# The v projection of a hybrid SSD / gMLP step by four weight tiles at once, and the order of the convolution tiles around it

## What is computed

```python
h = rms_norm(x, norm_w) * (1 + scale[:, None]) + shift[:, None]
proj = h @ w_in
xbc_raw, z_m, dt_raw, u_raw, v_raw, z_g, gl_m, gl_g = jnp.split(proj, _split_points(IN_SIZES), axis=-1)
y_m, h_fin = _ssd_branch(xbc_raw, dt_raw, z_m, h0, ...)   # xbc = silu(_dwconv(xbc_raw, conv_w, conv_b)), 5 taps
y_g = _gmlp_branch(u_raw, v_raw, z_g, ...)                # v = layer_norm(gelu(v_raw))
merged = sigmoid(gl_m) * (y_m @ w_out_m) + sigmoid(gl_g) * (y_g @ w_out_g)
return x + gate[:, None] * (merged @ w_out), h_fin
```

## Time and profile before

| | us |
|---|---|
| median of 3 runs | 1444.05 (1443.5 to 1444.36) |
| the profiled execution, its own time | 1443.57 |
| its span, first to last instruction | 1441.8 |
| PE busy | 1425.8, 99% of the span |
| DVE, POOL, ACT busy | 975.0, 1023.6, 474.2 |
| mean granted TensorE clock | 0.998 of full speed |

### The profile page before, as it was taken

The page is one execution under the profiler, slowest core; times in us unless marked ns, Lnnn a source line. Parts: engine busy times, 40 slices in busy tenths (PEclk is TensorE's granted clock), DMA queues, the critical chain, the costliest instruction groups (busy, mean ns, idle before and its releaser), DMA issues.

```text
span 1441.8 us, 27057 instructions
## 1 busy us (share of the span) xinstructions
PE 1425.8 (99%) x10191; PEld 1388.0 (96%) x10191; DVE 975.0 (68%) x1454; ACT 474.2 (33%) x1086; POOL 1023.6 (71%) x1421
## 2 busy tenths in 40 slices
PE   8999999999999999999999999999999999999997
PEld 5999998999999999999999999989999999999997
DVE  5865576674767678988879676567566876867234
ACT  4331223313766333001243323241257661320122
POOL 2688875596555589998859897658765556979772
PEclk9999999999999999999999999999999999999999
DMA  9112333113565565444332232421346565453222
GB/s 358 60 64 78 129 106 121 63 62 116 152 193 183 158 253 194 152 151 138 115 132 74 78 122 93 134 63 59 103 127 181 170 189 186 161 187 118 74 74 88
DMA packets 113838, 189.54 MB, mean 131 GB/s; under 512 B 12736, under 2 KB 76352, under 8 KB 112320
## 3 DMA queue, kind: packets, MB, share of 16 engines
q1 hardware_dynamic: 42736, 138.34, 29.1%
q10 hardware_dynamic: 70992, 49.63, 11.5%
HBM read 169.79 MB, written 18.15 MB: 130 GB/s over the span
## 4 chain that ended last, share of the span: by engine, by line
PE 96%; DVE 2%; DMA 1%; SPq 0%; ACT 0%; issue 0%; DVEq 0%; ACTq 0%
PE acc L600 78%; PE acc L567 6%; PE X L840 2%; PE X L805 2%; PE X L567 1%; PE X L825 1%; PE X L872 1%; DMA ada_pre<-in_wada 1%; PE X L851 1%; PE X L759 1%; DVE cv L1620 1%; PE X L649 0%; PE acc L718 0%; DVE h_pre L1473 0%; DVE xr L1936 0%; PE X L812 0%
## 5 line engine op out<-in xcount | busy, mean ns | idle before, releaser
L510 POOL CAST w_hi<-w_st 128x256 fp32r<-128x256 f32 x704 | 419.8, 610 | 396.1 <-issue 182.6
L514 POOL TENSOR_TENSOR w_lo<-w_st,w_hi 128x256 fp32r<-128x256 f32 x704 | 641.5, 921 | 0.0
L600 PE MATMUL acc<-h_hi,w_hi 128*128 128x320 f32 x1744 | 406.3, 314 | 0.7 <-ACT h_hi L1045 0.7
L600 PE MATMUL acc<-h_lo,w_hi 128*128 128x320 f32 x1744 | 397.8, 309 | 1.1 <-DVE h_lo L1467 1.1
L600 PE MATMUL acc<-h_hi,w_lo 128*128 128x320 f32 x1744 | 397.2, 309 | 0.0
L600 PEld LDWEIGHTS acc<-h_hi,w_hi 128*128 128x128 f32 x1744 | 288.6, 188 | 10.5 <-issue 7.8
L600 PEld LDWEIGHTS acc<-h_lo,w_hi 128*128 128x128 f32 x1744 | 291.3, 188 | 1.8 <-DVE h_lo L1467 1.7
L600 PEld LDWEIGHTS acc<-h_hi,w_lo 128*128 128x128 f32 x1744 | 291.7, 188 | 0.0
L1620 DVE SCALAR_TENSOR_TENSOR cv<-raw,convw_sb,cv 128x642 f32<-128x642 f32 x128 | 134.9, 1054 | 4.5
L1387 DVE SCALAR_TENSOR_TENSOR ada_acc<-ada_st,sc,ada_acc 128x512 f32<-128x512 f32 x112 | 104.2, 969 | 1.8
L1141 ACT ACTIVATE cvt<-cv 128x642 f32<-128x642 f32 x32 | 23.8, 743 | 158.4 <-DVE cv L1620 158.4
(11 more groups left out here) (257 smaller groups left out, 2474.8 us busy)
## 6 DMA issues: line engine op xcount, KB each, us to landing
w_st<-in_wts SPq DMA_DIRECT2D x176, 512.0 KB, 3.6
cum_bc<-cum_dram ACTq DMA_DIRECT2D x80, 256.0 KB, 4.9
ada_st<-in_wada SPq DMA_DIRECT2D x33, 512.0 KB, 4.3
ex_bc<-ex_dram ACTq DMA_DIRECT2D x64, 128.0 KB, 3.2
ada_pre<-in_wada SPq DMA_DIRECT2D x15, 512.0 KB, 9.7
mga_dram<-c_buf SPq DMA_DIRECT2D x16, 320.0 KB, 6.0
xf<-xf_dram SPq DMA_DIRECT2D x4, 1280.0 KB, 7.7
mga<-mga_dram SPq DMA_DIRECT2D x2, 2560.0 KB, 10.0
```

The source lines that it names most:

```text
L510: nc.gpsimd.tensor_copy(quarter(w_hi, slot, q), quarter(w_st, slot, q)).then_inc(s_pool, 1)
L514: nc.gpsimd.tensor_tensor(quarter(w_lo, slot, q), quarter(w_st, slot, q), f(quarter(w_hi, slot, q)), ALU.subtract).then_inc(w_split, 1)
L600: last = mm(a[:, hf, 0:n1], w[:, s, cols], x[:, k, hf * HALF:hf * HALF + n1], start=(k == 0 and n == 0), stop=(k == KC - 1 and n == 2))
```

## The change

- **v by four.** v's tiles are taken in two groups of four, in slots 3 to 6 and 20 to 23. 512 weight columns move in each matmul; a slot has a quarter of the rows of all four tiles, 2 blocks x 5 chunks x 3 = 30 matmuls. Each chunk of tokens fills a whole bank: chunk 4 X[1] or X[3], chunks 0 and 1 one accumulator, chunks 2 and 3 the other one. The chunks are taken in the order 4, 0, 1, 2, 3, and the wait for an accumulator stands ahead of its first chunk. A slot of v now waits for all four quarters of its weights.
- **ACT** applies the gelu bank by bank (`v_gelu`), 5 instructions of 512 columns a group, as each chunk of the last slot ends.
- **Convolutions.** CONV_AT becomes slots 0 to 2 and 7 to 19. For convolutions 4 to 15 (AHEAD) DVE does the first tap of convolution i + 1 ahead of the closing product of convolution i. ACT's order stays.
- **Transposes and bursts.** X sets in slots 15 to 22 at step 2; bursts 0, 1, 2 in slots 17 to 19 at step 3, the other 18 in slots 24 to 29.

```diff
-V_AT = (3, 4, 9, 10, 15, 16, 22, 23)
+V_AT = (3, 4, 5, 6, 20, 21, 22, 23)
+VQ = 4
+AHEAD = tuple(range(NRAW + 1, NCONV))
-A_AT = [(18 + a, 2) for a in range(7)] + [(25 + a // 3, 2 + 3 * (a % 3)) for a in range(14)]
-X_AT = [(p + 2, 4) for p in CONV_AT[8:14]] + [(24, 3), (24, 6)]
-V_BANK = (1, 1, 3, 1)
+A_AT = [(17 + a, 3) for a in range(3)] + [(24 + n // 8, n % 8 + 1) for n in (1 + 13 * a // 5 for a in range(18))]
+X_AT = [(p + 3, 2) for p in CONV_AT[8:16]]
+V_BANK = (1, 3)
...
+            bank = X[V_BANK[n % NQ]]
+            if i == 0:
...
+                if n % NQ == 1:
+                    pe.wait_ge(cum_ready, t // NT + 1)
+                    pe.wait_ge(s_out, NU * (t // NT) + 2)
+            pe.wait_ge(w_split, WQ * (t + 1))
...
+                for c in (NCH - 1,) + tuple(range(NCH - 1)):
+                    key = t0 if c < 2 else ("v", t0)
+                    if k == 0 and c in (0, 2):
+                        acc_ready(key)
+                    out = bank if c == NCH - 1 else acc_of(key)[:, c % 2, :]
+                    for m, (w, x) in enumerate(((w_hi, h_hi), (w_lo, h_hi), (w_hi, h_lo))):
+                        last = mm(out[:, :].rearrange("p (t n) -> p t n", t=VQ), x[:, k, P * c:P * (c + 1)],
+                                  w[:, t % 2, :].rearrange("p (t k n) -> p k t n", t=VQ, n=P)[:, kk, :, :],
+                                  start=(k == 0 and m == 0), stop=(k == KC - 1 and m == 2))
...
+                    last = A(v_tok[:, VQ * q:VQ * (q + 1), c, :], bank[:, :].rearrange("p (g n) -> p g n", n=P),
+                             ACT.Gelu_apprx_tanh)
+                    if c in (1, NCH - 2):
+                        free(key, last)
...
             for i in range(NCONV):
...
-                own.link(TS(o, r[:, PAD:PAD + CW], w[:, PAD:PAD + 1], w[:, TAPS:TAPS + 1], ALU.mult, ALU.add))
+                if i not in AHEAD:
+                    first_tap(i)
                 for tap in (0, 1, 3, 4):
...
+                if i + 1 in AHEAD:
+                    first_tap(i + 1)
                 dve.wait_ge(cvt_ready, NCONV * L + i + 1)
...
-                for a in {10: (0, 1), 11: (2,), 12: (3,), 13: (4,), 14: (5, 6), 15: (7, 8)}.get(i, ()):
+                for a in {11: (0, 1), 13: (2,), 15: (3,)}.get(i, ()):
                     a_unit(a)
```

More of the change, by code:

```diff
@@ L66, in accumulator_uses @@
             t = L * NT + p
-            if p in V_AT[1::2]:
+            if p in V_AT and p not in V_AT[::VQ]:
                 uses[t] = uses[t - 1]
@@ L71, in accumulator_uses @@
             at = 1 - at
+            if p in V_AT:
+                take(("v", t))
+                at = 1 - at
             if p == 0:
@@ L542, in acc_ready, with v_tile @@
                 pe.wait_ge(acc_free[at], n)
[L544 to L554, removed]
-                    pe.wait_ge(hpre_ready, 8 * (ready[2] + 1))
[L556 to L559, removed]
+        def v_tile(t, i, ready=None, hooks=()):
+            t0 = t - i
+            n = NQ * (t // NT) + V_AT.index(t0 % NT) // VQ
+            bank = X[V_BANK[n % NQ]]
+            if i == 0:
+                if n % NQ == 0 and ready is not None:
+                    pe.wait_ge(hpre_ready, 8 * (ready[2] + 1))
+                if n % NQ == 1:
+                    pe.wait_ge(cum_ready, t // NT + 1)
+                    pe.wait_ge(s_out, NU * (t // NT) + 2)
+            pe.wait_ge(w_split, WQ * (t + 1))
+            step = 0
+            for kk in range(2):
+                k = 2 * i + kk
                 if ready is not None:
@@ L562, in v_tile @@
                         pe.wait_ge(r, 8 * ready[2] + k + 1)
[L563 to L571, removed]
+                for c in (NCH - 1,) + tuple(range(NCH - 1)):
[7 more added lines that the diff above has]
+                                  start=(k == 0 and m == 0), stop=(k == KC - 1 and m == 2))
+                    if kk == 1 and c == NCH - 2:
                         last.then_inc(tile_done, 1)
+                    elif k == KC - 1:
+                        last.then_inc(v_done, 1)
+                    step += 1
                     for at, hook in hooks:
-                        if (at == 2 * i + 1 and c == 2) or (at == 2 * i + 2 and c == NCH - 1):
+                        if (5 * at + 3) // 4 == step:
                             hook()
@@ L1141, in conv_tanh, with v_gelu @@
                 A(cvt[:, 0:CW], cv[:, i % 2, 0:CW], ACT.Tanh).then_inc(cvt_ready, 1)
+            def v_gelu(q, t):
+                t0 = t - VQ + 1
+                own.link(A(warm[:, :], eps_sb[:, :], ACT.Gelu_apprx_tanh))
+                for i, c in enumerate((NCH - 1,) + tuple(range(NCH - 1))):
+                    key = t0 if c < 2 else ("v", t0)
+                    if i < NCH - 1:
+                        act.wait_ge(v_done, (NCH - 1) * (NQ * L + q) + i + 1)
+                    else:
+                        act.wait_ge(tile_done, t + 1)
+                    bank = X[V_BANK[q]] if i == 0 else acc_of(key)[:, c % 2, :]
+                    last = A(v_tok[:, VQ * q:VQ * (q + 1), c, :], bank[:, :].rearrange("p (g n) -> p g n", n=P),
+                             ACT.Gelu_apprx_tanh)
+                    if c in (1, NCH - 2):
+                        free(key, last)
+                evacuated(act, ("v", t0))
+                act.sem_inc(v_made, 1)
             def copies(p):
@@ L1151, in _ @@
                 t = T0 + p
-                if L == 0 or p >= RAWT:
+                if p in V_AT and V_AT.index(p) % VQ == VQ - 1:
+                    v_gelu(V_AT.index(p) // VQ, t)
+                elif L == 0 or p >= RAWT:
                     act.wait_ge(tile_done, t + 1)
                 if p in V_AT:
[L1155 to L1162, removed]
                     if L > 0 and p == RAWT + 1:
@@ L1607, in a_unit, with first_tap @@
                 last.then_inc(xw_ready, 1)
-            for i in range(NCONV):
-                ch = (i + 8) % NCONV
+            def first_tap(i):
                 if L > 0 and i < NRAW:
```

31 lines of the change are left out of this document (18 added, 13 removed).

## The result

| | us |
|---|---|
| median of 4 runs of the changed kernel | 1466.60 (1465.19 to 1469.04) |
| median of before beside them, 4 runs | 1443.78 (1443.41 to 1444.36) |
| ratio | 1.0155, 95% interval [1.0143, 1.0167] |
| the profiled execution of after, its own time; its span | 1469.04; 1467.3 |
| mean granted TensorE clock in that execution | 0.991 |

The change makes the kernel 22.8 us slower. The profiled execution is 2.4 us above the median, and its opening, which the change doesn't touch, is 2.3 us longer than before up to slot 3 of layer 0 (that slot starts at 65.12 and not at 62.86). In that opening PE's clock was at half twice, 16.5 to 20.0 and 40.4 to 43.8 us, where the profile of before shows it full. The other three runs, with a mean granted clock of 0.993, are shorter. I leave these 2.3 us out of what follows and count from slot 3 on.

A forecast was written before the change was run, and what follows sets the result against it. PE's own time was taken to bound the kernel. Wider matmuls -6.4, copy-out waits +4.9 and +14.7, and late weight quarters +1.3 gave +14.5 on 1444.05, hence 1458.5 us; the range was 1443 to 1467.5.

The forecast's parts named there:

- rival 3: Matmuls of 512 columns in v's slots are no cheaper than two of 256; +20.9 us, 1465; chance 0.06.
- rival 4: PE's clock halves behind a 5 to 8 us pause in slot 20: 4.5 us a layer, +23.5, 1467.5; chance 0.08.
- Wider matmuls: PE, 16 slots of v: 30 matmuls at 0.227 us, read off a line through three sizes, save 6.4 us.
- The loop: DVE and ACT, first tap to first tap: closing product and handover add 0.87, giving 7.55 us in layer 0, 8.04 in layer 1.
- Waits for the copy-out: PE waits for ACT's accumulator copy-outs up to slot 19's, mostly in slot 20: 4.9 us in layer 0, 14.7 in layer 1.
- All four quarters: Slots 4 and 5 of layer 1 start late behind POOL's last weight quarter: 1.3 us for both, bounds 0 and 2.1.
- The cover that I named for slot 20: In slots 20 to 23 the copy-out wait covers the wait for POOL's weight quarters, so no time was added there.
- Rival 1: The convolution loop never holds PE and only the wider matmuls count; 1437.7 us; chance 0.12.
- Rivals 2: Short convolution loops and matmuls without a fixed part: -3.0, 1441.0 us, or +3.4, 1447.5 with 6.4 saved; chance 0.08.

The follow-up runs named there:

- experiment 3: The changed kernel with ACT's copy-out of convolution tile i + 1 ahead of the tanh of convolution i; 1442.65 us, ratio to before 0.9989.
- experiment 5: The changed kernel with 20 and 24 further 512-column matmuls, products thrown away, ahead of slot 20 of each layer; 1461.58 us, ratio to before 1.0125.
- experiment 7: The changed kernel with the copy-out ahead of the tanh, plus POOL's weight quarters in the order 0, 2, 1, 3; 1438.66 us, ratio to before 0.9963.
- experiment 4: The changed kernel with chunks 4, 0, 1 of both row blocks first in slots 3 and 20, taking the second accumulator later; 1460.06 us, ratio 1.0115.
- experiment 1: The changed kernel with AHEAD empty, so DVE does the closing product ahead of the next first tap again; 1445.29 us, ratio to before 1.0008.
- experiment 8: The changed kernel with POOL's quarters in the order 0, 2, 1, 3 and the old order of taps and copy-out; 1442.75 us, ratio 0.999.
- experiment 6: The changed kernel with the copy-out ahead of the tanh, plus the first row block of v's slots waiting for three quarters only; 1440.09 us, ratio 0.9972.

## Why the prediction was right, and which terms were off

Forecast +14.5, measured +22.8; the time of 1466.6 is in the range, near its high end. The mechanism of the waits was right, but the range held for another reason: the bounds of the forecast proper end at 1464.4, and only the room given to rivals 3 and 4, 0.14 between them, reaches to 1467.5. Rival 4 is what happened on top of the forecast. Step by step:

- **Wider matmuls, -6.4: right.** 0.227 us a matmul and 6.80 a slot in the trace, in every slot of v where nothing else is in the way. The line through three sizes in the earlier trace rows held for a fourth. The Trainium skill ("TensorE: Matmul & The Clock Gate", Back-to-back issue gap) would give an estimated 0.216, a saving of 11.6; the trace disagrees.
- **The loop, 7.55 and 8.04: right in kind, a little short in both layers.** 7.51 and 7.60 us are among the shortest of layer 0, 7.70 and 8.02 of layer 1 (828.80 to 836.50 to 844.52). But in layer 0 the first ones are longer: 107.60 to 115.91 is 8.31, since the first tap takes 1.07 there and the four taps 4.87, beside a busy POOL. From 107.60 to 198.34, 11 loops with 5.2 us of other work among them, the mean is 7.78. 11 x 0.23 = 2.5 us is about what the wait of layer 0 was short. In layer 1 the same count (816.82 to 915.82, 9.0 us of other work) gives a mean of 8.18, and 11 x 0.14 = 1.5 us.
- **Waits for the copy-out, 4.9 and 14.7: measured 7.2 and 16.0** (2.5 + 4.7, 10.5 + 5.5). Place and pattern as forecast: in layer 1 from slots 11 and 12 on, the largest in slot 20. In layer 0 the two slots before slot 20 had a share. Not in the sum was the state copy ahead of slot 20, 0.4 and 0.9 of these.
- **All four quarters, 1.3: measured 0.9**, and I had placed it in slots 4 and 5. Most of it is in slot 3 (0.66). The cover that I named for slot 20 was real: as soon as experiment 3 removed the wait for the copy-out, the wait for POOL came out in front of it, 1.1 us in layer 0 and 1.6 in layer 1.
- **The clock: the step that failed.** I gave the sum no term for it and kept it as rival 4, with a chance of 0.08. But it doesn't exclude the forecast: a pause of 5 us in slot 20 was part of the forecast itself, and what PE's clock does behind such a pause belonged in the same sum. The earlier trace rows had shown the clock at half where PE has nothing to do. Rival 4 priced it at 4.5 us a layer, all 21 matmuls; measured are 14 and 12 matmuls at 0.427, 2.9 and 2.5 us. With the rule of the Trainium skill ("TensorE: Matmul & The Clock Gate", HAM oscillation: idle stretches between groups of matmuls bring the throttle back) this trace agrees, as experiment 5 shows by filling the pause.

The difference of 8.3 us is thus the clock 5.4, the waits 3.6, POOL -0.4, and -0.3 that I can't assign.

Rival 1 (PE is never held, 1437.7) is ruled out for this kernel by the trace. Experiments 3 and 7 show it where ACT's order is changed, as rival 1 had asked. Rivals 2 and 3 are out: the loops were not short and the matmuls not dear.

What is left open: why the clock fell behind the 2.09 us at 848.7 in experiment 4 and not behind the 2.64 of layer 0, and over what POOL and DVE get into each other's way.

## What to carry to other kernels

When an instruction is moved ahead on one engine, look up what it waits for and where that stands in the queue of the engine that makes it: an order that is right on DVE alone may close a loop over ACT. Two swapped lines on ACT turned 22.8 us lost into 1.2 gained. And if a forecast has PE stand still for some microseconds, what the clock costs behind the pause belongs in the sum, since the same pause brings both. Once such a wait is gone, ask at once which engine's lateness it was hiding.

## What the runs showed of the hardware

- **A matmul at half clock shows no fixed part.** At 2.4 GHz a matmul of 512 columns with fresh weights starts every 0.227 us: 0.213 for the columns by the 0.417 ns of the earlier trace rows, and 0.013 that is left over. At 1.2 GHz it starts every 0.427, just twice the 0.213. In the earlier sizes the 0.013 was there each time.
- **Work that is thrown away can save time.** 44 further matmuls, 10 us of PE, made the kernel 5.0 us faster, for they kept the clock up through a pause that was there anyhow.
- **The length of a pause alone doesn't tell whether the clock falls.** It fell to half at the end of one of 2.09 us (848.70, experiment 4) and stayed up behind 2.64 us in the same execution and behind 2.09 us at the same place of the changed kernel. With the five pauses of 3.2 to 5.5 us in slot 20 (changed kernel twice, experiments 1, 4 and 8) it fell each time: within the pause for 4.67 and 5.54 us, at most 1.2 us after PE had begun again for the other three.
- **POOL and DVE slow each other down.** In the kernel of experiment 7, POOL in order of time: a cast and a subtraction alone, then both beside DVE's taps:

```profile
210.15 0.40 POOL L518 CAST w_hi<-w_st 128x256 fp32r<-128x256 f32 x1
210.51 0.74 POOL L522 TENSOR_TENSOR w_lo<-w_st,w_hi 128x256 fp32r<-128x256 f32 x1
...
843.95 0.99 POOL L518 CAST w_hi<-w_st 128x256 fp32r<-128x256 f32 x1
844.91 1.32 POOL L522 TENSOR_TENSOR w_lo<-w_st,w_hi 128x256 fp32r<-128x256 f32 x1
```

A tile's eight pieces take 4.2 us alone (tiles 23 and 24) and up to 8.6 beside DVE, more than a slot of 7.04. By slot 15 of layer 1 the last quarter is ready 4.9 us into the slot that uses it. This is where the waits for POOL in experiments 3, 6 and 7 come from. In that trace none of the 167 casts that no DVE instruction overlaps takes over 0.41 us, and none of the 150 subtractions over 0.75. It goes the other way too: in the changed kernel DVE's first tap is at most 0.62 where POOL does nothing (5 of them) and up to 1.18 beside POOL, and each of the other taps 0.89 (19 of them) against up to 1.36. This overlap has its share in the loops of layer 0 that were longer than forecast.
